# A two-layer hybrid mixer and expert kernel: five tiles projected together in layer one, and another placing of the projections beside the expert tiles in layer two

## The reference

```python
mod = silu(cond) @ w_ada + b_ada                 # six rows per group: prompt, sample
u = ln(x) * (1 + sc1) + sh1
mix, new_state = mixer(u, state)                 # u @ w_in (3136 wide), convolution, three scans, gates, w_out
x = ln(alpha * x + g1 * mix) * ln1_w + ln1_b
u = ln(x) * (1 + sc2) + sh2
x = ln(alpha * x + g2 * peer(u)) * ln2_w + ln2_b
```

## Time and profile before

| What | Value |
|---|---|
| Median of 3 runs | 5011.3 us (5007.21 to 5012.49) |
| Profiled execution | 5011.9 us, of which the span of its instructions 5010.1 us |
| PE busy | 3883.2 us, 78% |
| DVE busy | 2917.3 us, 58% |
| ACT busy | 1155.8 us, 23% |
| POOL busy | 1543.5 us, 31% |
| DMA | 1607.89 MB, 321 GB/s on average, 67.5% of the 16 engines' time for the gathers' queue |
| Granted PE clock, mean | 0.908 of full speed |

### The profile page before, as it was taken

How to read it: one execution, slowest core, us unless ns; L and a number is a source line. 1 busy time by engine, 2 the same in 40 slices (tenths; PEclk the granted TensorE clock), 3 DMA queues, 4 the chain that set the end, 5 groups by cost and what they waited for, 6 DMA issues and landing times.

```text
span 5010.1 us, 40096 instructions
## 1 busy us (share of the span) xinstructions
PE 3883.2 (78%) x12076; PEld 1947.8 (39%) x12076; DVE 2917.3 (58%) x6886; ACT 1155.8 (23%) x2937; POOL 1543.5 (31%) x1416
## 2 busy tenths in 40 slices
PE   8873997866887877976776699786678788787776
PEld 3431474542343432433443246553334333243222
DVE  1245325647676686684456542464767768668555
ACT  0101234411212212222421222341122221221211
POOL 0101122212434344443222312221244444434443
PEclk9986998888999999998888899887899999999999
DMA  8564775576999999999877957556599999999998
GB/s 289 180 230 182 257 263 187 201 272 259 404 386 413 400 391 420 376 398 367 326 307 274 363 206 275 200 184 249 213 406 388 412 406 380 421 383 401 390 421 358
DMA packets 314585, 1607.89 MB, mean 321 GB/s; under 512 B 41633, under 2 KB 82849, under 8 KB 144385
## 3 DMA queue, kind: packets, MB, share of 16 engines
q0 software_dynamic: 184320, 1342.26, 67.5%
q1 hardware_dynamic: 129952, 262.99, 14.6%
q10 hardware_dynamic: 96, 0.10, 0.0%
HBM read 1568.02 MB, written 37.20 MB: 320 GB/s over the span
## 4 chain that ended last, share of the span: by engine, by line
PE 42%; DMA 23%; DVE 19%; issue 6%; SPq 4%; ACT 3%; POOL 2%; POOLq 1%; DVEq 0%; ACTq 0%
PE bank L1924 20%; DMA big<-in_experts,big 19%; DVE big L1328 5%; PE bank L1678 4%; PE bank L1673 4%; PE bank L1904 3%; PE bank L1627 2%; POOL big L2030 2%; PE bank L1875 2%; ACT big L1578 1%; DVE big L1246 1%; DVE big L1248 1%; SPq L831 1%; DVE big L1245 1%; DMA big<-in_w_in 1%
## 5 line engine op out<-in xcount | busy, mean ns | idle before, releaser
L1924 PE MATMUL bank<-big 128*128 128x512 f32 x5120 | 2569.7, 652 | 866.0 <-ACT big L1578 846.9
L2030 POOL DMA_INDIRECT big<-in_experts,big x1280 | 1439.0, 1124 | 3169.2 <-PE bank L1924 2803.5
L1924 PEld LDWEIGHTS bank<-big 128*128 128x128 f32 x5120 | 1023.1, 207 | 2317.9 <-ACT big L1578 1171.0
L1328 DVE CUSTOM_DVE_ANT_0 big<-big 128x1024 f32<-128x1024 f32 x1280 | 1546.1, 1226 | 592.0 <-DMA big<-in_experts,big 591.2
L1578 ACT ACTIVATE big<-big 128x128 f32<-128x128 f32 x1280 | 445.1, 395 | 1261.7 <-DVE big L1316 1238.0
L1588 ACT ACTIVATE big<-big 128x2 f32<-128x2 f32 x640 | 130.9, 204 | 1470.6 <-DVE big L1328 1470.0
L1316 DVE TENSOR_TENSOR big<-big 128x2 f32<-128x2 f32 x640 | 103.3, 161 | 312.6 <-ACT big L1588 261.0
L1678 PE MATMUL bank<-big 128*128 128x256 f32 x960 | 220.8, 387 | 16.3 <-DMA big<-in_w_in 15.1
L1673 PE MATMUL bank<-big 128*128 128x128 f32 (+1 forms) x768 | 214.8, 435 | 1.4 <-DMA big<-in_w_in 1.4
L1678 PEld LDWEIGHTS bank<-big 128*128 128x128 f32 x960 | 185.3, 194 | 56.8 <-DMA big<-in_w_in 17.4
L1627 PE MATMUL bank<-big 128*2 128x512 f32 x384 | 175.9, 613 | 18.9 <-DMA big<-in_b_ada 11.1
(11 more groups left out here) (240 smaller groups left out, 2805.8 us busy)
## 6 DMA issues: line engine op xcount, KB each, us to landing
big<-in_w_ada SPq DMA_DIRECT2D x24, 2048.0 KB
big<-in_w_in SPq DMA_DIRECT2D x48, 1024.0 KB, 7.1
big<-in_experts,big POOLq DMA_INDIRECT x1280, 10.1
big<-modd SPq DMA_DIRECT2D x34, 512.0 KB, 24.2
big<-in_w_out SPq DMA_DIRECT2D x4, 4096.0 KB, 20.0
big<-in_peer_wq SPq DMA_DIRECT2D x4, 4096.0 KB, 38.8
y_d<-big SPq DMA_DIRECT2D x20, 512.0 KB, 5.5
big<-y_d SPq DMA_DIRECT2D x20, 512.0 KB, 11.1
```

Source lines behind the costliest of these rows:

```text
L1328: v_.tensor_tensor_reduce(ring[:, j, 0:D], ring[:, j, 0:D], EU[it % 2], 1.0, 0.0, ALU.mult, ALU.add, DOT[:, n % 16:n % 16 + 1]).then_inc(e ...
L1924: i = mm(ps[4 + h][:, :], DG[:, n % DIAGS * P:(n % DIAGS + 1) * P], ring[:, n % RING, D + 512 * h:D + 512 * h + 512], start=(n == 0), stop ...
L2030: g_.indirect_dma_start(ring[:, n % RING, :], None, io["experts"], bass.IndirectOffsetOnAxis(ap=IDX[it % 2].bitcast(U32)[:, n:n + 1], axis ...
```

## The change

The list of phases is written out, with the sets of tiles that are projected together (`BATCHES`) and convolved together (`CONVS`). In layer one all five tiles are projected at once, ahead of the first scan, with no experts beside them; the prompt tile stands beside the four samples in matmuls of its own (128 or 256 columns, banks 4 and 5, and bank 7 for the small block) behind each matmul group of the four. In layer two the prompt's projection, scan and then tile 2's mixers run beside tile 1's experts, and the prompt's mixers (tile 5) with the projection of samples 1 to 3 run beside tile 4's. Sample 4 is projected beside tile 5, and the convolution of all four samples follows it; none follows batch 2. The last rows of the plan are as before. Twelve chunks of the modulation are placed before the first projection's last x and twelve beside the first scan and the prompt's mixers; the side tile's small block waits for the twelfth. The staging buffers fall from three to two, Z and ZA share memory with X and U, and the turned convolution rows of the samples use one bank instead of two. The mixer phases are (0), (1), (2, 3, 4), (5) and (6 to 9), so the output and query weights are loaded five times instead of four; `w_in` is loaded four times as before. The number of phases and barriers stays twelve.

By their weights the steps fall so: tile 0's 60 spread steps 32 in the scan and 28 in tile 1's mixers; tile 1's 51 spread steps 16, 8 and 27 in projection, scan and mixers; tile 4's 51 spread steps 22 in the prompt's mixers and 29 in the projection; tile 5's 53 spread steps 11, 23 and 19. The diff, cut to its core:

```diff
+BATCHES = ((0, (0, 1, 2, 3, 4)), (1, (0,)), (1, (1, 2, 3)), (1, (4,)))
+CONVS = ((0, (0, 1, 2, 3, 4)), (1, (0,)), (1, (1, 2, 3, 4)))
+PHASES = (("ip", (0,)), ("sc", 0), ("mx", (0,)), ("sc", 1), ("mx", (1,)), ("ip", (1,)), ("sc", 2), ("mx", (2, 3, 4)),
+          ("mx", (5,)), ("ip", (2, 3)), ("sc", 3), ("mx", (6, 7, 8, 9)))
+IP_PHASES = [_k for _k, _p in enumerate(PHASES) if _p[0] == "ip"]
+MX_PHASES = [_p[1] for _p in PHASES if _p[0] == "mx"]
...
+FIRST_MODS = 12
...
+def split(b):
+
+
+    n = len(BATCHES[b][1])
+    side = 1 if b == 0 else 0
+    return n, side, n - side
...
+def conv_of(b):
+
+
+    return (0, 1, 2, 2)[b], b != 2
...
+def ci_col(b, s):
+
+
+    return 1 + P * s if b == 1 or s == 0 else (130 if b == 0 else 1) + P * (s - 1)
...
+    for ph, (kind, arg) in enumerate(PHASES):
+        ticks.append((("go", ph), 3.0))
+        for b in arg if kind == "ip" else ():
+            n, side, m = split(b)
+            ticks.append((("ip", b, "go"), 1.0))
+            for i in range(n):
+                ticks.append((("ip", b, f"x{i}"), 6.0))
+            late = []
+            beside = {3: ["smt"], 4: ["g1"], 5: ["g2"], 6: ["zz", "cv0"], 7: ["cv1", "cv2"], 8: ["cv3", "cv4"], 9: ["cv5"]}
...
+                    ticks.append((("ip", b, f"b{j}.{h}"), (1.8 * n if BLOCKS[j] in FEAT else 3.5 * n / len(halves(b, j))) if j else 4.0))
...
-    a, b = TICK["sc", 0, "met"], TICK["mx", 0, "met"]
-    spread_over(order, 0, a, [("mod", u) for u in range(4, 16)])
-    spread_over(order, a + 1, b, [("mod", u) for u in range(16, MODS)])
-
-    def tile(it, first, last, g0, g1):
-
+    spread_over(order, 0, TICK["ip", 0, "x4"], [("mod", u) for u in range(4, FIRST_MODS)])
+    order.append(("m", TICK["go", 1]))
+    spread_over(order, TICK["go", 1] + 1, TICK["met", 2], [("mod", u) for u in range(FIRST_MODS, MODS)])
+    start = TICK["met", 2] + 1
+    ends = (("mx", 1, "smd"), ("mx", 2, "smd"), ("mx", 3, "smd"), ("met", 7), ("ip", 2, "end"), ("mx", 6, "smd"),
+            ("mx", 7, "smd"), ("mx", 8, "smd"), ("met", 11))
+    for it, end in enumerate(ends):
+        g0, g1 = 7 if it else 0, 60 if it in (0, 5) else 58
         order.extend(("e", it, g) for g in range(g0))
-        if last >= first:
-            spread_over(order, first, last, [("e", it, g) for g in range(g0, g1)])
+        spread_over(order, start, TICK[end], [("e", it, g) for g in range(g0, g1)])
         order.extend(("e", it, g) for g in range(g1, PAIRS))
-
...
+        start = TICK[end] + 1
+    order.extend(("e", 9, g) for g in range(PAIRS))
...
-        UT = a(KC * 512).rearrange("p (k n) -> p k n", k=KC)
+        UT = a(KC * 640).rearrange("p (k n) -> p k n", k=KC)
...
+        XU = a(3 * D)
+        X, U = [XU[:, 0:D], XU[:, D:2 * D]], XU[:, 2 * D:3 * D]
+        Z, ZA = XU[:, 0:5 * 2 * NDIR], XU[:, 5 * 2 * NDIR:10 * 2 * NDIR]
...
+        STG = [a(5 * 260) for _ in (0, 1)]
...
+        def stage_free(eng, b, k):
+
+            if k >= 2:
+                eng.wait_ge(p_st[k % 2], staged(b, k - 2))
+            elif b:
+                eng.wait_ge(p_st[k % 2], staged(b - 1, 8 - k))
...
+        def mix_phase(t):
+
+
+            m = [t in tiles for tiles in MX_PHASES].index(True)
+            return m + 1, t == MX_PHASES[m][0]
...
+                    if i >= 3:
+                        sp.wait_ge(p_xs[i % 2], 16 * ((i - 1) // 2))
+                        sp.sem_inc(passed, 1)
+                    sp.dma_start(X[i % 2], x_in[s]).then_inc(p_x[i % 2], 16)
+                    if s:
+                        sp.wait_ge(n_pe.sem, n_pe.at(t - 1, "tr1"))
+                        sp.sem_inc(passed, 1)
+                        sp.dma_start(U, pos_in[s - 1]).then_inc(p_pos, 16)
+
+                if not opens:
+                    sp.wait_ge(z_dve.sem, z_dve.at(b - 1, "dt"))
+                    sp.sem_inc(passed, 1)
                 load_x(0)
...
+                else:
+                    sp.wait_ge(p_pe.sem, p_pe.at(b - 1, "b11.1"))
+                    sp.sem_inc(passed, 1)
                 load_w(1)
...
+                            if side:
+                                pe.wait_ge(m_dve, FIRST_MODS)
+                                for k in range(KC):
+                                    mm(ps[7][0:64, 0:P], WS[:, k, :], UT[:, k, 0:P], start=(k == 0), stop=(k == KC - 1))
                             for k in range(KC):
-                                i = mm(ps[6][0:64, 0:n * P], WS[:, k, :], UT[:, k, 0:n * P], start=(k == 0), stop=(k == KC - 1))
...
                             for k in range(KC):
-                                i = mm(out[:, 0:n * P], w[:, k, h * P:(h + 1) * P], UT[:, k, 0:n * P],
+                                i = mm(out[:, 0:m * P], w[:, k, h * P:(h + 1) * P], main[:, k, :],
                                        start=(k == 0), stop=(k == KC - 1))
+                            if side:
+                                beside_free(b, j, h)
+                                for k in range(KC):
+                                    i = mm(ps[4 + h][:, 0:P], w[:, k, h * P:(h + 1) * P], UT[:, k, 0:P],
+                                           start=(k == 0), stop=(k == KC - 1))
...
+                            if side and h == 0:
+                                beside_free(b, j, h)
+                                for k in range(KC):
+                                    i = mm(ps[4 + j % 2][:, 0:256], UT[:, k, 0:P], w[:, k, :], start=(k == 0), stop=(k == KC - 1))
...
+            def beside_free(b, j, h):
+
+
+                if BLOCKS[j] in FEAT and j >= 2:
+                    by = p_dve if j - 1 < 4 else p_act
+                    pe.wait_ge(by.sem, by.at(b, f"s{j - 1}.{h}"))
+                elif BLOCKS[j] not in FEAT:
+                    for i, q in ((j - 2, 0), (j - 1, j % 2)):
+                        if BLOCKS[i] in FEAT:
+                            pe.wait_ge(p_act.sem, p_act.at(b, f"s{i}.{j % 2}"))
+                    if BLOCKS[j - 2] not in FEAT:
+                        by = p_dve if BLOCKS[j - 2] in ("gv", "mv") else p_act
+                        pe.wait_ge(by.sem, by.at(b, f"s{j - 2}.0"))
...
+                    pe.wait_ge(c_act.sem, c_act.at(v, f"silu{c}"))
+                    if c:
+                        pe.wait_ge(c_act.sem, c_act.at(v, f"tok{c - 1}"))
                     else:
-                        pe.wait_ge(z_dve.sem, z_dve.at(r, "z0b" if n > 2 else "z0a"))
-                    for q in range(n):
-                        i = turned(ps[6 + c % 2][:, q * P:(q + 1) * P], CO[c % 2][:, q * P:(q + 1) * P], ident)
+                        pe.wait_ge(z_dve.sem, z_dve.at(b, f"z0{gate_groups(b) - 1}"))
+                    for q, s in enumerate(tiles):
```

More of the change, by code:

```diff
@@ L70, in tick_table @@
+def ci_col(b, s):
+    return 1 + P * s if b == 1 or s == 0 else (130 if b == 0 else 1) + P * (s - 1)
+CONV_W = (5 * P + 1, P, 4 * P)
 def tick_table():
     ticks = []
[L73 to L97, removed]
@@ L384, in build, with evicted @@
-        p_st = [sem(f"p_st{k}") for k in range(3)]
+        p_pe = mk("p_pe", [in_proj_names(b) for b in B])
+        def evicted(b, kinds):
+            names = []
+            for j, name in enumerate(BLOCKS):
+                if name not in kinds:
+                    continue
+                if name == "mv":
+                    names.append("one")
+                for h in halves(b, j):
+                    if split(b)[1] and (h == 0 or name in FEAT):
+                        names.append(f"s{j}.{h}")
+                    names.append(f"e{j}.{h}")
+            return names
@@ L389, in build @@
+        c_pe = mk("c_pe", [[f"t{c}" for c in range(5)]] * 3)
         c_st = [sem(f"c_st{i}") for i in (0, 1)]
@@ L811, in mix @@
                         sp.dma_start(dst, src).then_inc(o_ld.sem, 16)
-                    if s == tiles[0]:
+                    if first:
                         for dst, src in PARAMS_A[0:2]:
@@ L815, in mix @@
                         sp.dma_start(wo, io["w_out"][l].rearrange("(k p) n -> p k n", p=P)).then_inc(o_wo, 16)
-                    if s != tiles[0]:
+                    if not first:
                         sp.wait_ge(q_pe.sem, q_pe.at(t - 1, "s3"))
@@ L978, in gates @@
+            def gates(b):
+                l, tiles = BATCHES[b]
+                n = len(tiles)
+                v = conv_of(b)[0]
+                link = linker(ve, z_dve, b)
                 w = 2 * NDIR
@@ new lines, in gates @@
+            def gates(b):
+                n, side, m = split(b)
+                v = conv_of(b)[0]
+                w = n * 2 * NDIR
+                link = linker(ae, z_act, b)
+                yield TICK["ip", b, "e0.0"]
+                if b != 3:
+                    ae.wait_ge(p_par, 128 * (v + 1))
+                    i_act.take(v, "ea")
+                    a_.activation(ALOG, ALOG, ACT.Exp).then_inc(i_act.sem, 1)
+                ae.wait_ge(p_pe.sem, p_pe.at(b, "b0.0"))
+                if side:
+                    a_.activation(SMF[:, 0:P], ps[7][0:64, 0:P], ACT.Copy)
```

(4 more changed lines are left out.)

812 lines of the change are left out of this document (404 added, 408 removed).

## The result

The changed kernel took 5122.19 us (median of 4 runs, 5118.92 to 5127.85) against 5011.9 us of the kernel before, run beside it (4 runs, 5007.21 to 5013.12): ratio 1.0223, 95% interval 1.0205 to 1.0241. The forecast was 5072, range 4985 to 5140. So the sign was right and the time is inside the range, but the loss is 110 us where 60 were worked out. A run can be granted a lower clock than the others of its kernel; in the experiments one was, 5562.15 us at 0.693 in a kernel whose other three took 4919.9 to 4927.35 us, and it is left out there.

What follows compares the result with a forecast made beforehand. Gathers bind where one tile's mixers stand beside experts, elsewhere the mixers' own chain, with steps inserted in it. 208 - 272 + 43 + 192 - 111 = +60 on a span of 5010.1: about 5072 us, range 4985 to 5140.

Steps and rivals of the forecast that it cites:

- part 1: First projection, five tiles with no experts beside them: 381 us in place of 173.3, +208 (bounds 345 and 410).
- part 4: Tile 1's mixers take 28 expert steps instead of 15: 211.0 us against 168.2, +43 (35 to 50).
- part 6: Tiles 2 and 3: unchanged, 0.
- part 7: From tile 4's mixers to tile 6's: 1260 us in place of 1371.0, -111 (-145 to -75).
- Part 5: Prompt's second projection, scan and tile 2's mixers beside tile 1: 526 us in place of 333.6, +192 (180 to 205).
- part 3: Four-tile projection gone; scan after it: 13 start, 41.7 a tile, 32 steps at 5.6, 359 us; -272.
- Part 2: First scan and prompt mixers, 238.0 us, twelve modulation chunks beside them before and after: 0, bounds -8 and +8.
- Denser steps keep PE at its upper clock: Scans and mixers with more steps: each step costs up to 1.7 us less, 111 in all, 4961 us; chance 0.12.
- The gathers hide the prompt's stages: Beside tile 1, which stays near 344 us: part 5 falls from 192 to about 10, total 4890 us; chance 0.05.
- New waits: Two staging buffers: stores delayed 4 us in each of nine blocks of three batches add 108, 5180 us; chance 0.12.
- No change: Parts 1 and 3 both at their low bounds (345 and 318): total 5000 to 5020 us; chance 0.09.

Runs made afterwards that it cites:

- the delay: Changed kernel with each step's value matmuls issued one step later on TensorE and GpSimd fetching one pair less ahead: 4975.28 us, 0.9919 of the kernel before.

## Why the prediction was right, and where it was not

**Right in sign and in where the steps went.** The steps of the old projection did not vanish; they went where a step costs more. Parts 1, 4, 6 and 7 were off by 10, 7, 5 and 14 us. In part 1 the x stage was as worked out (small block at 141.2 us for 139) and so was the barrier (366.8 to 371.6, five us); blocks and convolution rows took 225.6 us, against 182 + 50 + 5 = 237.

**Luck in the sums.** Part 5 came out at 525.9 of 526, but its four rows were 8 us over, 17 under, 7 over and 2 over (70.6, 135.5, 106.6 and 213.2 against 63, 152.6, 99.6 and 211.0). In part 7 three tiles' projection took 292.4 us for 275 and tile 9's 138.4 for 117, while the row of thirteen steps, 94.9 us in the sum, was 36.0 with seven: 35 of tile 4's steps stood beside the projection, not 26. These errors cancel too. So the time lies inside the range although the loss was nearly twice the one worked out, and of the 47 us between them part 3 makes 50.

**The step that failed is the price in part 3**, "I stay with 5.6, on which three rows agree". On the same base of 13 + 4 x 41.7 it was (409.3 - 180) / 32 = 7.2 us a step, 50 us in all. The three rows did not agree, they were used up: two gave the price, from a difference of two steps, and the third gave the base. Near the counts that it came from the price held: the scan with 22 steps took 305.8 us for the 306 of part 7. From 18 to 32 steps each added step cost (409.3 - 280.7) / 14 = 9.2 us. With the delay the same two counts give (296.3 - 240.2) / 14 = 4.0. So the price that rises with the density is the meeting: a wait of up to 9.1 us before matmuls that then take 5.2 us a step, not the matmuls alone, which the prediction had taken for the whole of it though the wait, 41.8 us in 18 steps, stood in the trace of the kernel before.

**Part 2, "0, bounds -8 and +8", was 5 us outside.** There were twelve chunks as said, but a chunk's price depends on where it stands (9.6 us beside the scan, 3.7 beside the mixers). With three beside the scan and nine beside the mixers, in place of four and eight, these prices give 6 us less than before, not 13.1 more. Nearly all of it is in the mixers, 169.3 us against 157.7 (253.6 to 411.3): there PE's longest wait for SP's queue is 11.0 us after and 5.7 before; what makes the rest stays open. The first scan, with one chunk less, did not get shorter (81.8 us against 80.3), at a granted clock of 0.81 against 0.89.

**The rivals.** *Denser steps keep PE at its upper clock*: in the scans this was not seen, 0.83 in the dense scan against 0.85 in the thinner one, and 0.85 with 22 steps as with 16. With the waits gone the same steps were granted 0.89: PE was busy 298.37 of 409.30 us in the one and 253.24 of 296.30 in the other. The Trainium skill (TensorE: Matmul & The Clock Gate, section on the HAM clock gate) says that activity releases the throttle; these two runs agree with it. The mistake was to take more steps for more activity, since in the scan they brought more waiting. In the mixers the rival's clock did come, from 0.80 to 0.85 in tile 1's with 28 steps for 15 and from 0.78 to 0.82 in tile 6's with 19 for 13, but these stretches were no shorter than forecast (218.2 us for 211, 185.6 for 184). *The gathers hide the prompt's stages*: 525.9 us, not some 344. *New waits*: there was none of weight at the staging buffers (ScalarE waited three times for a store, 4.4, 3.9 and 2.1 us, where 108 were reckoned); the wait that grew, at the values, was an old one. *No change*: no part was at the bounds that it needed.

## What to carry to other kernels

When work of one stream is inserted in another's chain, look at whether all engines handle the same item at the same place in their orders: then every item is a meeting, and here its price grew with the density. Issuing the last engine's part one item later costs buffers and some late release, so it pays only where waits, not transfers, set the pace. A price fitted on two near counts should not be carried to nearly twice the count, and an order should be judged again when the price has changed: the same new layer one lost 43 us with dear steps and won 35 with cheap ones.

## What was not expected

Stretches bound by the gathers are not bound by them alone. In the one run with half the value matmuls left out, tiles 2 and 3 took 660.4 us (1689.5 to 2349.9) against 689.9, though PE's granted clock was 0.80 there against 0.95 and the gathers' number the same; the gathers' 360.3 us of waiting for line 2029 to free a buffer fell to 317.9. So a slot's turn includes TensorE's part. That fits the 16 us which the delay cost those tiles; no run here separates the two.
